# First block of a two-block transformer kernel re-ordered: convolution groups behind each GLA head, local attention between gate groups

## The reference, cut to what matters

```python
u = rmsnorm(h, g_mix)
gq, gk, gv, gr, ga, cx, cb, cc, sq, sk, sv, gates = split_columns(u @ w_in)
log_a = log_sigmoid(ga @ gla_w_alpha + gla_b_alpha) / 16
o = gla_chunked(gq, gk, gv, log_a)            # 4 heads of 128, chunks of 64
y_gla = (rms(o) * gla_norm_g * silu(gr)) @ w_gla_o
y_conv = (cb * causal_dwconv(cc * cx, conv_w)) @ w_conv_o          # 512 channels
y_swa = swa_sink_attention(sq, sk, sv, sinks, slopes) @ w_swa_o
                      # 8 query heads, 2 kv heads of 64, window 128, ALiBi, a sink
gt = sigmoid(gates)                           # 3 x 1024 columns
merged = gt[0] * y_gla + gt[1] * y_conv + gt[2] * y_swa
h = h + merged @ w_o
h = h + (silu(a) * b) @ w_down                # a, b: convolved halves of rmsnorm(h) @ w_up
```

## Time and profile before

| | us |
|---|---|
| median of 3 runs | 2066.83 (2065.13 to 2070.43) |
| the profiled execution | 2072.34 |
| its span, first to last instruction | 2070.6 |
| TensorE busy | 1903.6 (92%) |
| VectorE busy | 929.8 (45%) |
| ScalarE busy | 720.7 (35%) |
| GpSimd busy | 695.3 (34%) |

### The profile page before, as it was taken

How to read it: one execution, slowest core, us unless ns; L and a number is a source line. 1 busy time by engine, 2 the same in 40 slices (tenths; PEclk the granted TensorE clock), 3 DMA queues, 4 the chain that set the end, 5 groups by cost and what they waited for, 6 DMA issues and landing times.

```text
span 2070.6 us, 26890 instructions
## 1 busy us (share of the span) xinstructions
PE 1903.6 (92%) x11004; PEld 1648.5 (80%) x11004; DVE 929.8 (45%) x1424; ACT 720.7 (35%) x1034; POOL 695.3 (34%) x290
## 2 busy tenths in 40 slices
PE   5978886999998999999789999879999889999997
PEld 3766665788886888888689999868888789999886
DVE  3343344322225566521354545554565455555301
ACT  4444322222224333323335555332233243333221
POOL 2222211344443444444222323211323234444442
PEclk9988978999999999999989999889999899999998
DMA  4112110232232333333121212111211122333331
GB/s 156 55 51 61 51 51 31 64 100 92 94 91 78 94 94 96 96 94 99 51 70 54 62 62 72 52 42 41 62 52 55 58 72 93 92 92 93 93 99 63
DMA packets 44185, 154.15 MB, mean 74 GB/s; under 512 B 5776, under 2 KB 6032, under 8 KB 44064
## 3 DMA queue, kind: packets, MB, share of 16 engines
q1 hardware_dynamic: 44064, 152.44, 23.8%
HBM read 150.33 MB, written 2.10 MB: 74 GB/s over the span
## 4 chain that ended last, share of the span: by engine, by line
PE 77%; DVE 14%; ACT 6%; issue 1%; ACTq 1%; SPq 0%; DMA 0%; DVEq 0%
PE ps L547 75%; DVE arena L1171 5%; ACT arena L825 4%; PE ps L551 2%; DVE arena L1178 1%; DVE full L1312 1%; DVE u_lo L1168 1%; ACT L830 1%; DVE arena L1168 1%; DVE arena L1525 1%; ACTq L1151 1%; DVE arena L1403 0%; DVE v_hi L1186 0%; DVE h_res L1358 0%; DVE arena L1484 0%
## 5 line engine op out<-in xcount | busy, mean ns | idle before, releaser
L521 POOL TENSOR_TENSOR w_lo<-w_raw,w_hi 128x1024 fp32r<-128x1024 f32 x280 | 687.4, 2455 | 1323.4 <-ACT w_hi L825 1323.2
L547 PE MATMUL ps<-u_hi,w_hi 128*128 128x264 f32 (+3 forms) x2376 | 667.6, 335 | 32.4 <-DVE u_lo L1168 29.8
L547 PE MATMUL ps<-u_hi,w_lo 128*128 128x264 f32 (+3 forms) x2376 | 655.4, 330 | 0.0
L547 PE MATMUL ps<-u_lo,w_hi 128*128 128x264 f32 (+3 forms) x2376 | 652.8, 328 | 0.0
L547 PEld LDWEIGHTS ps<-u_hi,w_hi 128*128 128x128 f32 (+1 forms) x2376 | 408.0, 195 | 89.3 <-issue 34.7
L547 PEld LDWEIGHTS ps<-u_lo,w_hi 128*128 128x128 f32 (+1 forms) x2376 | 406.1, 194 | 38.7 <-issue 0.8
L547 PEld LDWEIGHTS ps<-u_hi,w_lo 128*128 128x128 f32 (+1 forms) x2376 | 407.4, 194 | 36.6 <-issue 1.0
L825 ACT ACTIVATE w_hi<-w_raw 128x1024 fp32r<-128x1024 f32 x280 | 297.0, 1061 | 234.2 <-PE ps L547 198.9
L547 PE MATMUL ps<-arena 128*64 128x128 f32 (+9 forms) x1212 | 184.7, 304 | 53.5 <-ACT arena L825 28.0
L547 PEld LDWEIGHTS ps<-arena 128*128 128x128 f32 (+4 forms) x1212 | 161.4, 189 | 78.1 <-issue 34.5
L1178 DVE SCALAR_TENSOR_TENSOR ffn<-ps,par,ffn 128x512 f32<-128x512 f32 (+2 forms) x176 | 132.0, 750 | 192.9 <-ACT ffn L825 187.7
(11 more groups left out here) (128 smaller groups left out, 1610.1 us busy)
## 6 DMA issues: line engine op xcount, KB each, us to landing
w_raw<-weights SPq DMA_DIRECT2D x280, 512.0 KB, 3.6
h_res<-xT SPq DMA_DIRECT2D x4, 512.0 KB, 5.5
outT<-h_res SPq DMA_DIRECT2D x8, 256.0 KB, 2.1
cst<-consts SPq DMA_DIRECT2D x1, 992.0 KB, 9.6
par<-params SPq DMA_DIRECT2D x1, 243.5 KB, 7.4
msk<-cmask SPq DMA_DIRECT2D x1, 64.0 KB, 10.1
h_res<-metaT SPq DMA_DIRECT2D x1, 64.0 KB, 9.5
arena<-w_alpha SPq DMA_DIRECT2D x1, 32.0 KB, 10.0
```

The lines of the kernel that those rows point to most:

```text
L521: nc.gpsimd.tensor_tensor(w_lo[:, s % SPL, 0:n], w_raw[:, s % RAW, 0:n], w_hi[:, s % SPL, 0:n], ALU.subtract).then_inc(w_lo_ok, 1)
L547: return nc.tensor.matmul(out, lhsT, rhs, start=start, stop=stop)
```

## The change

- The three convolution groups of tile h stand behind `gr(h)` of GLA head h. `prep(h)` stays behind `gr(h)`, `head_a(h)` comes behind `cb(h)`, and b, c, d behind the next head's `gq`, `gk`, `gv` (behind `sk`, `sv`, `sq(0)` for the last).
- The merge runs over branches 0 and 1 for all 8 tiles first, then over branch 2. Attention unit n stands there: `swa_a(n)` behind `gate(n,0)`, `swa_b(n)` behind `gate(n,1)`, `swa_c(n)` behind `y(n,1)`. The partial sums of all 8 tiles stay in `mrg`, which has 11 tiles instead of 5.
- An attention unit is now two query heads of both kv heads. Score matmuls alternate between partitions 0 to 63 and 64 to 127 of the inputs, with outputs in two banks; products with the values alternate between the lower and upper 64 output partitions.
- The gate is a tanh of half the value; VectorE makes (tanh + 1) times `y`, twice the gated value, and `wo` is added with a factor 0.5.
- `prep` writes its two in-place products last; `gq(i)` waits for `st_a` (TensorE through `head_a`) instead of `ready`.

The diff, cut to its core:

```diff
+MERGE = [(m, br) for m in range(KD) for br in range(2)] + [(m, 2) for m in range(KD)]
...
     for h in range(GLA_H):
-        for name in ("gq", "gk", "gv", "gr"):
+        for name in ("gq", "gk", "gv", "gr", "cc", "cx", "cb"):
             full(name, h, "w_in", o[name] + h * P)
...
-    for t in range(CONV_T):
-        for name in ("cc", "cx", "cb"):
-            full(name, t, "w_in", o[name] + t * P)
-    for m in range(KD):
-        for br, matrix in enumerate(("w_gla_o", "w_conv_o", "w_swa_o")):
-            full("gate", (m, br), "w_in", o["gates"] + br * D + m * P)
-            full("y", (m, br), matrix, m * P, "y%d" % br, 4)
+    for m, br in MERGE:
+        full("gate", (m, br), "w_in", o["gates"] + br * D + m * P)
+        full("y", (m, br), ("w_gla_o", "w_conv_o", "w_swa_o")[br], m * P, "y%d" % br, 4)
...
+    for h in range(GLA_H):
+        put("gr", h, ("prep", h))
+        put("cb", h, ("head_a", h))
+        rest = [(k, h + 1) for k in ("gq", "gk", "gv")] if h + 1 < GLA_H else [("sk", 0), ("sv", 0), ("sq", 0)]
+        for stage, where in zip("bcd", rest):
+            put(*where, ("head_" + stage, h))
...
-    fill = [(n, t) for t in range(CONV_T) for n in ("cc", "cx", "cb")]
-    stages = [(s, 2 * b + g) for b in range(NBLK) for g in range(SWA_G) for s in ("swa_a", "swa_b", "swa_c")]
-    for n, st in enumerate(stages):
-        put(*fill[min(n // 2, len(fill) - 1)], st)
+    for n in range(SWA_G * NBLK):
+        put("gate", (n, 0), ("swa_a", n))
+        put("gate", (n, 1), ("swa_b", n))
+        put("y", (n, 1), ("swa_c", n))
...
-        mrg = sb("mrg", [P, 5, SEQ], F32, s1)
+        mrg = sb("mrg", [P, KD + 3, SEQ], F32, s1)
...
             def swa_a(n):
-                b, g = n // SWA_G, n % SWA_G
+                b, th = n // SWA_G, n % SWA_G
...
-                for t in range(SWA_T):
-                    col = 4 * BANK + 256 * t
-                    last = mm(pf[:, col + c0:col + 256], s_q[lo, t, b * BLK:(b + 1) * BLK],
-                              s_k[lo, (b - 1) * BLK + c0:(b + 1) * BLK])
+                for i in range(2):
+                    for g in range(SWA_G):
+                        lo = slice(SWA_HD * g, SWA_HD * (g + 1))
+                        col = (4 + g) * BANK + 256 * i
+                        last = mm(pf[:, col + c0:col + 256], s_q[lo, 2 * th + i, b * BLK:(b + 1) * BLK],
+                                  s_k[lo, (b - 1) * BLK + c0:(b + 1) * BLK])
...
             def swa_c(n):
-                for t in range(SWA_T):
+                for i in range(2):
                     js = range(1 if b == 0 else 0, 2)
+                    at = (2 * th + i) * BLK
                     for j in js:
-                        last = mm(ps[lo, 3, t * BLK:(t + 1) * BLK], s_vtok[:, b - 1 + j, lo], s_PT[:, t, j, :],
-                                  start=(j == js[0]), stop=(j == 1))
+                        for g in range(SWA_G):
+                            lo = slice(SWA_HD * g, SWA_HD * (g + 1))
+                            last = mm(ps[lo, 3, at:at + BLK], s_vtok[:, b - 1 + j, lo], s_PT[:, 2 * g + i, j, :],
+                                      start=(j == js[0]), stop=(j == 1))
...
                 elif kind == "gq":
                     if i:
-                        act.wait_ge(ready, i)
+                        act.wait_ge(st_a, i)
...
-                    f(mrg[:, 3 * ((3 * m + br) % 2), :], x, ACT.Sigmoid).then_inc(free, 1)
+                    f(mrg[:, KD + n % 2, :], x, ACT.Tanh, scale=0.5).then_inc(free, 1)
...
                 elif kind == "y":
                     m, br = i
                     evacuated(dve, g - 1)
-                    gate = mrg[:, 3 * ((3 * m + br) % 2), :]
-                    mul(mrg[:, 2 if br else 1, :], x, gate).then_inc(free, 1)
-                    dve.wait_ge(free, TURN[g] + 1)
+                    gate, part, more = mrg[:, KD + MERGE.index(i) % 2, :], mrg[:, m, :], mrg[:, KD + 2, :]
+                    twice_silu(more if br else part, gate, x).then_inc(free, 1)
                     if br:
-                        link(tt(mrg[:, 1, :], mrg[:, 1, :], mrg[:, 2, :], ALU.add))
+                        dve.wait_ge(free, TURN[g] + 1)
+                        last = tt(part, part, more, ALU.add)
                     if br == 2:
-                        parts(m_hi[:, m, :], m_lo[:, m, :], mrg[:, 1, :])
+                        link(last)
+                        parts(m_hi[:, m, :], m_lo[:, m, :], part)
+                elif kind == "wo":
+                    c0, c1 = columns(g)
+                    tile = h_res[:, i, c0:c1]
+                    madd(tile, x, 0.5, tile).then_inc(free, 1)
...
-                    mul(g_qE, qf1, ge[:, 0, :])
-                    mul(g_kE, kf1, ge[:, 1, :])
...
+                    mul(qf1, qf1, ge[:, 0, :])
+                    mul(kf1, kf1, ge[:, 1, :]).then_inc(ready, 1)
```

More of the change, by code:

```diff
@@ L190, in put @@
         after[GROUP_OF[(kind, idx)]].extend(what)
[L192 to L206, removed]
+    for h in range(GLA_H):
[4 more added lines that the diff above has]
+            put(*where, ("head_" + stage, h))
+    names, tail = ("hf", "hq", "hi", "hg"), (("dt", 0), ("mb", 0), ("mb", 1), ("mc", 0))
+    for h in range(HG_H):
+        at = [(k, h + 1) for k in names] if h + 1 < HG_H else tail
+        put(names[3], h, ("prep", GLA_H + h))
+        nxt = [(k, h + 2) for k in names] if h + 2 < HG_H else tail if h + 2 == HG_H else (("mc", 1),)
+        for stage, where in zip("abcd", list(at[1:4]) + [nxt[0]]):
+            put(*where, ("head_" + stage, GLA_H + h))
     for g in after:
@@ L355, in program @@
         take, at = carve(arena1[:, :])
-        ge = take(4, SEQ)
+        ge = take(3, SEQ)
         gt1, gt2, gcum = take(SEQ), take(SEQ), take(SEQ)
-        g_qE, g_kE = take(SEQ), take(SEQ)
         g_kZ, g_qZ = take(NBLK, BLK), take(NBLK, BLK)
@@ L362, in program @@
         g_attn, g_ktok, g_vtok, g_state = (take(NBLK, BLK) for _ in range(4))
-        g_o, g_osq, g_or = take(SEQ), take(SEQ), take(SEQ)
+        g_o, g_osq = take(SEQ), take(SEQ)
         g_gate = take(2, SEQ)
         ga_sb, wal = take(SEQ), take(GLA_H * P)
+        c_c, c_y, c_a = take(SEQ), take(SEQ), take(SEQ)
+        c_u = take(SEQ + 2)
         g_D, negb = take(NBLK), take(GLA_H)
[L367 to L379, removed]
+        s_q = take(SWA_T, SEQ, at_=0)
+        s_k, s_vf = take(SEQ, at_=4 * SEQ), take(SEQ, at_=5 * SEQ)
+        s_vtok = take(NBLK, P, at_=6 * SEQ)
+        s_small = take(8, SWA_T, at_=7 * SEQ)
+        s_L = take(SWA_T, 256, at_=8 * SEQ)
+        s_P = take(SWA_T, 256, at_=10 * SEQ)
+        s_PT = take(SWA_T, 2, BLK, at_=12 * SEQ)
         take, at = carve(arena2[:, :])
@@ L636, in head_a @@
                         c = GLA_C
-                        mm(ps[:, 4, at:at + c], g_kE[:, at:at + BLK], g_qE[:, at:at + c])
+                        mm(ps[:, 4, at:at + c], kf1[:, at:at + BLK], qf1[:, at:at + c])
                         mm(ps[0:c, 4, at + c:at + BLK], g_kL[:, b, :], g_qB[:, b, :])
-                        mm(ps[c:BLK, 4, at + c:at + BLK], g_kE[:, at + c:at + BLK], g_qE[:, at + c:at + BLK])
+                        mm(ps[c:BLK, 4, at + c:at + BLK], kf1[:, at + c:at + BLK], qf1[:, at + c:at + BLK])
                         turn(ps[:, 5, at:at + BLK], g_kZ[:, b, :])
@@ L898, in group @@
                 elif kind == "cc":
-                    if i == 0:
-                        act.wait_ge(tile_lo, TILE_NO[("y", GLA_H - 1)])
-                    else:
+                    if i:
                         evacuated(act, GROUP_OF[("cx", i - 1)])
@@ L1028, in prep @@
                     f(ge[:, 2, :], ge[:, 2, :], ACT.Exp, scale=s)
-                    f(ge[:, 3, :], gcum, ACT.Exp, scale=-s).then_inc(exp_ok, 1)
+                    f(gcum, gcum, ACT.Exp, scale=-s).then_inc(exp_ok, 1)
                 else:
@@ L1069, in head_d @@
                 if n < GLA_H:
-                    last = root(g_or, ps[:, 6, :], P)
+                    last = root(g_osq, ps[:, 6, :], P)
                 else:
@@ L1377, in prep @@
                     cum = gcum.rearrange("p (c t) -> p c t", t=GLA_C)
-                    e = [ge[:, j, :].rearrange("p (c t) -> p c t", t=GLA_C) for j in range(4)]
+                    e = [ge[:, j, :].rearrange("p (c t) -> p c t", t=GLA_C) for j in range(3)]
                     tt(e[0], cum, bc(cum[:, :, GLA_C // 2 - 1], GLA_C), ALU.subtract)
@@ L1399, in prep @@
                     mul(g_kZ[:, :, 0:GLA_C], g_kL, bc(d[:, :, 1], GLA_C))
-                    mul(g_qZ[:, :, GLA_C:], g_qB, bc(d[:, :, 0], GLA_C)).then_inc(ready, 1)
+                    mul(g_qZ[:, :, GLA_C:], g_qB, bc(d[:, :, 0], GLA_C))
+                    mul(qf1, qf1, ge[:, 0, :])
+                    mul(kf1, kf1, ge[:, 1, :]).then_inc(ready, 1)
                     return
@@ L1468, in head_d @@
                 i = n if gla else n - GLA_H
-                o, r, gate = (g_o, g_or, g_gate) if gla else (h_o, h_or, h_gate)
```

(6 more changed lines are left out.)

36 lines of the change are left out of this document (15 added, 21 removed).

## The result

The changed kernel takes **1979.35 us** (median of 4 runs, 1978.7 to 1980.24) against 2066.09 us for the kernel before beside it (4 runs, 2065.13 to 2070.43): ratio 0.9577, 95% interval 0.956 to 0.9593, 86.7 us less. The prediction was 1973, range 1955 to 1997. The profiled execution took 1978.91 us, its span is 1977.1.

What follows compares the result with a forecast made beforehand. Bound: TensorE, with 158.7 us of stages, idle and low clock in heads and attention. This becomes 24.5 + 22.5 + 16.4 + 1 = 64.4, winning 94.3: 2072.3 to 1978.0, less 5.5 for the median, predicted 1973, range 1955 to 1997.

Steps and rivals of the forecast that it cites:

- What bounds it, and the cover: Heads and attention: 60.5 us of TensorE idle plus low clock, removed by putting groups of matmuls before the waiting stages.
- The new stall before `cb`: Heads: weight slab late behind `prep` in ScalarE's queue, 2.4 us idle before each `cb`, 9.6 in all, plus 6.8 low clock.
- `prep`'s products still end inside `cb`.: Heads: VectorE's products end 16.5 us after the tanh, under the 17 us cover, so `head_a` itself waits no more.
- Stages: TensorE's short head and attention steps at full clock: 24.5 us for four heads, 22.5 us for attention.
- The seams: Attention: about 12 more transitions between groups and stages, 0.07 us each, 1 us in all.
- The pairs: Attention: score and product matmuls on different array halves run together, saving 12.2 us.
- Rival 2: Attention: paired matmuls run one after the other, 12.2 us more, 1985; chance 0.10.
- The softmax chain: Attention, scores to transposes: 7.09 us, covered by 8.4 us of `y` and `gate` matmuls with 1.3 to spare; one table load.
- Rival 4: Attention: the chain from scores to transposes outlasts its 8.4 us cover, eight stalls, 26 us more, 1999; chance 0.13.
- Rival 5: Attention: clock stays low around the short stages though idle is gone, 20 us come back, 1993; chance 0.05.
- rivals 3 and 6: 3: slab in time or clock stays up, 1957, chance 0.10. 6: ScalarE starves TensorE in gates, over 2073, chance 0.02.
- The sum: Whole kernel: 94.3 us won, profiled 2072.3 becomes 1978.0; median of runs 5.5 lower, 1972.5, predicted 1973.

Runs made afterwards that it cites:

- The attention half alone: Kernel before with only the attention part of the change (paired units between gate groups, partial sums kept); convolution groups stay behind all heads: 2000.59 us, ratio 0.9668.
- mid-`prep` split: Changed kernel with ScalarE splitting `cb`'s weight slab inside `prep`, while it waits for VectorE's scan, instead of after `prep`: 1985.51 us, ratio 0.9598.
- the version with the slab first and the hold: Changed kernel with `cb`'s slab split at the start of `prep`, and ScalarE waiting for `prep`'s products before splitting later slabs: 1969.95 us, ratio 0.9529.
- the version with the hold: Changed kernel with one wait more: ScalarE waits for `prep`'s products before splitting the next slab in `cx`; `cb`'s slab stays late: 1978.92 us, ratio 0.9574.

## Why the prediction was right, and where it was not

**What bounds it, and the cover.** Right. By the waits, 60.5 us of idle became 9.5. The heads: 168.14 us became 211.45 - 67.8 (the 12 convolution groups) = 143.7, 24.5 won, 25.5 predicted. Attention to `w_o`: 160.09 - 67.8 + 248.04 = 340.3 became 158.43 + 114.04 = 272.5, 67.9 won, 68.8 predicted. The attention half alone gave 3.3 of 4.2 per cent, 78% (76% against the first median of the kernel before), where the prediction has 68.8 of 94.3, 73%. One reason given for the heads was not needed: in the change the first head's products end at 76.30 and the next `gq` begins at 80.57, so its old wait for `ready` would have been met as well; it is the cover that took it off the path.

**The new stall before `cb`.** Right in place and size: 2.28 us four times, 2.4 predicted. Low clock followed three of four, not all: 3 x 1.7 = 5.1 us, not 6.8. That the slab's place behind `prep` in ScalarE's queue is the cause is shown by its removal: with the slab split first all four idles and the low clock behind them are gone. The waits do not show it as "released by GpSimd", as the prediction had it; one sees it in the timeline.

**"`prep`'s products still end inside `cb`."** Right in outcome, wrong in its number, and the weakest step. The 16.5 us from the tanh to the products' end were copied from the earlier trace rows, with one `w_lo` instruction beside them. Before, ScalarE then stood at its copy of `gq` and could split no more; the change took that block away, and so let two more `w_lo` instructions run beside the products. They took 9.91 us, and ended at 76.30, 20.7 after the tanh at 55.57. Without its idle `cb` would have begun at 67.93 and ended 5.65 later, at 73.6, so `head_a` would have waited 2.7 us; it waited little (0.4 us, once) because `cb` was itself 2.28 us late and mostly slow. Two faults hid one another, as the mid-`prep` split found out: it took the one away and met the other, 11.4 us.

**Stages.** `head_a` takes 3.13 us at full clock and not 2.70: half of a duration at half clock was too little for it, 1.7 us over four heads; what holds it is open. Scores 1.06, products 1.02 (1.03 predicted for both); transposes 0.79 (1.0 predicted). The seams were taken as 1 us and are bigger: 36 matmuls of `y` and `gate` between scores and transposes take 8.46 us for 8.37, a gate beside a stage 5.77 for 5.58, a `y` 2.97 for 2.79, so about 0.47 a round and 3.8 in all. So `head_a` and the seams cost 1.7 + 2.8 more than summed, the transposes (8 x 0.21) and the low clock that did not come 1.7 + 1.7 less, which leaves some 1 us; the spans differ by 0.8.

**The pairs.** Right, 13.4 us for 12.2, rows as well as columns. Rival 2 fell. That neighbours in issue order must belong to different halves was an assumption of mine; it is not needed for four passes and is for eight.

**The softmax chain.** Right: no idle before the transposes, a margin of 1.33 us where 1.3 was predicted, one table load in the gates. Rival 4's mechanism is real (28.9 us of idle once the transposes stand one group earlier) but does not set in. Rival 5 fell (clock 1.00), rivals 3 and 6 as well.

**The sum.** Predicted span 1976.3, measured 1977.1. The step that failed is the last: "the median of runs, 2066.83, is 5.5 lower: 1972.5". The 5.5 us were for the most part low clock in that one profiled execution of the kernel before, as its repetition shows (a span of 2065.2 on the same waits), and low clock there comes behind idle. The change takes the idle away, so there was nothing to subtract from its own time: its profiled 1978.91 is within 0.5 us of its median, and 0.9 from the 1978.0 of the step before. That most of the excess lay in low clock is shown (3.9 of 5.4 us in the attention stretch alone); that the change has none to give back is argued from its idle, and borne out by its own runs, 1978.7 to 1982.0 in both sets. Why an execution has more low clock is open.

## What to carry to other kernels

When work is moved under a stall, ask what the stalled engine could not do meanwhile: ScalarE's block had kept GpSimd quiet beside VectorE's longest chain, and its removal nearly doubled that chain. A cover is to be compared with the whole queue of each producer, weights included; the 16.5 us won here beyond the change came from three shifts within the queues of ScalarE and VectorE, with no work taken away. And a difference between one profiled execution and the median may belong to the stalls in it, as here, and then doesn't carry over to a kernel without them.

## What the runs showed of the hardware

**VectorE's products out of SBUF stand still beside GpSimd.** Nine products in `prep`, by the number of `w_lo` instructions (2.47 us each) beside them: 3.50 us with none, 5.53 with one, 7.87 with two, 9.91 with three, so some 2.1 us for each. VectorE's groups over the products, by shape (busy us, mean ns), of the change and of the version with the slab first and the hold:

```profile
L1165 DVE TENSOR_TENSOR arena<-arena 128x256 f32<-128x256 f32 x6 | 6.5, 1125 | 2.3 <-ACT arena L822 2.3
L1165 DVE TENSOR_TENSOR arena<-arena 128x512 f32<-128x512 f32 x2 | 3.5, 1766 | 0.0
```

```profile
L1169 DVE TENSOR_TENSOR arena<-arena 128x256 f32<-128x256 f32 x6 | 2.3, 421 | 2.3 <-ACT arena L822 2.3
L1169 DVE TENSOR_TENSOR arena<-arena 128x512 f32<-128x512 f32 x2 | 1.3, 686 | 0.0
```

It is not an even slowing: a single product of 0.42 us took 2.46 where it met a `w_lo` instruction and 0.42 where it did not.

```profile
67.93 2.46 DVE L1165 TENSOR_TENSOR arena<-arena 128x256 f32<-128x256 f32 x1
```

The Trainium skill, "SBUF — State Buffer", SBUF: two separate sides, has it: VectorE with two SBUF inputs and a GpSimd instruction that reads SBUF share one pair of ports, which the first to start locks for its whole instruction. This trace agrees in kind and size: the product took a `w_lo` instruction's length (2.46 for 2.48). The prediction did not use it; with it and a count of the `w_lo` instructions that ScalarE would now let in, it could have seen that the 5.65 us of the earlier trace rows would not hold.

What reads PSUM is not held. In the last eight `gate` and `y` pairs with `w_o` of the change, 426 to 540 us, where GpSimd is busy 42% of the time, the products that read the `y` tile from PSUM take 0.69 us, while the casts out of SBUF take 1.47 on average (four at 0.43 and four at 2.51). Of all 24 such products of the merge, twelve started beside a `w_lo` instruction and twelve ran with none, at 0.69 us each.

```profile
L1176 DVE SCALAR_TENSOR_TENSOR mrg<-mrg,ps 128x512 f32<-128x512 f32 x9 | 6.2, 687 | 42.9 <-PE ps L541 42.9
L1180 DVE CAST m_hi<-mrg 128x512 fp32r<-128x512 f32 x8 | 11.8, 1471 | 0.3
```

The sum of 1.0 us and the cast of 1.5 us that the prediction took from the earlier trace rows are such averages, not prices of an undisturbed instruction.

**Equal idles, unequal clock.** An idle of 2.28 us in the same place was followed by 3.4 us at half clock in one execution and by none in the next, and so for the kernel before (7.83 or 5.78 us for one group). A price of 1.7 us for each such idle held three times in four in both executions of the change, and twice in four in the version with the hold.
